# Modulation of two token streams with the weights as TensorE's stationary operand, the gate's third computed later

## What is computed

```python
silu_c, silu_cc = jax.nn.silu(c), jax.nn.silu(c_ctx)          # two vectors of 1024
for l in range(DEPTH):                                        # DEPTH = 2
    mod_x = silu_c  @ w_ada[l] + b_ada[l]                     # w_ada[l]: 1024 x 3072
    mod_c = silu_cc @ w_ada[l] + b_ada[l]
    shift, scale, gate = jnp.split(mod, 3, axis=-1)           # for x and for the context
    h = rmsnorm(x, g_pre) * (1.0 + scale) + shift             # before the input projection
    y = merge(branches(h)) @ w_out                            # attention, conv, retention, Fourier
    x = x + gate * rmsnorm(y, g_post)                         # at the end of the layer
```

## Time and profile before

| | us |
|---|---|
| median of three runs | 2798.82 |
| lowest and highest run | 2790.05, 2798.84 |
| the profiled execution | 2791.78 |
| its span (first to last instruction) | 2790.0 |
| busy PE, loads of stationary operands (PEld) | 2569.3 (92%), 2123.9 (76%) |
| busy DVE, ACT, POOL | 1123.0, 1083.0, 1292.2 |
| mean granted TensorE clock | 0.974 |

### The profile page before, as it was taken

How to read it: one execution, slowest core, us unless ns; L and a number is a source line. 1 busy time by engine, 2 the same in 40 slices (tenths; PEclk the granted TensorE clock), 3 DMA queues, 4 the chain that set the end, 5 groups by cost and what they waited for, 6 DMA issues and landing times.

```text
span 2790.0 us, 39335 instructions
## 1 busy us (share of the span) xinstructions
PE 2569.3 (92%) x13000; PEld 2123.9 (76%) x13000; DVE 1123.0 (40%) x1675; ACT 1083.0 (39%) x2170; POOL 1292.2 (46%) x1012
## 2 busy tenths in 40 slices
PE   7888969988999899999999869888999899999998
PEld 2777957777888778888887358777888678888886
DVE  2453446386244233333331356474244323333322
ACT  2644553375212443333332333574212433343332
POOL 1667952365222355555554132464222455556553
PEclk9999989999999999999999979999998999999999
DMA  5346642100121143344336431000210233344333
GB/s 230 100 119 187 189 162 61 31 1 13 45 64 29 56 122 109 111 132 146 109 110 236 160 99 48 19 1 25 63 39 25 83 114 112 109 132 146 110 109 121
DMA packets 387918, 270.48 MB, mean 97 GB/s; under 512 B 15452, under 2 KB 360668, under 8 KB 385252
## 3 DMA queue, kind: packets, MB, share of 16 engines
q1 hardware_dynamic: 373792, 231.26, 27.5%
q10 hardware_dynamic: 14024, 37.88, 3.8%
HBM read 259.63 MB, written 9.45 MB: 96 GB/s over the span
## 4 chain that ended last, share of the span: by engine, by line
PE 58%; issue 19%; POOL 14%; DVE 5%; ACT 3%; POOLq 1%; DMA 0%; DVEq 0%; ACTq 0%; SPq 0%
PE ps L596 56%; POOL w_lo L509 14%; DVE a_probT_lo L1346 2%; PE ps L742 1%; ACT a_probT_hi L1130 1%; DVE a_out_sum L1346 1%; DVE norm_tmp L1423 1%; DVE hT_lo L1346 1%; DMA w_ada<-in_w_ada 0%; DVE r_prev L1616 0%; PE ps L694 0%; POOLq L508 0%; ACT square_junk L973 0%; PE ps L632 0%; ACT a_prob L1119 0%
## 5 line engine op out<-in xcount | busy, mean ns | idle before, releaser
L509 POOL TENSOR_TENSOR w_lo<-w_raw,w_hi 128x512 fp32r<-128x512 f32 x786 | 1055.3, 1350 | 1115.1 <-ACT w_hi L973 1104.8
L596 PE MATMUL ps<-hT_hi,w_hi 128*128 128x512 f32 (+1 forms) x2528 | 943.7, 373 | 50.6 <-POOL w_lo L509 27.0
L596 PE MATMUL ps<-hT_hi,w_lo 128*128 128x512 f32 (+1 forms) x2528 | 932.4, 369 | 0.0
L596 PE MATMUL ps<-hT_lo,w_hi 128*128 128x512 f32 (+1 forms) x2528 | 932.3, 369 | 0.0
L973 ACT ACTIVATE w_hi<-w_raw 128x512 fp32r<-128x512 f32 x786 | 492.0, 630 | 1063.5 <-PE ps L596 883.3
L596 PEld LDWEIGHTS ps<-hT_hi,w_hi 128*128 128x128 f32 x2528 | 481.1, 190 | 141.7 <-POOL w_lo L509 22.9
L596 PEld LDWEIGHTS ps<-hT_hi,w_lo 128*128 128x128 f32 x2528 | 481.6, 190 | 78.7
L596 PEld LDWEIGHTS ps<-hT_lo,w_hi 128*128 128x128 f32 x2528 | 482.0, 191 | 76.5
L1346 DVE TENSOR_TENSOR merge_tmp<-merge_tmp,ps 128x512 f32<-128x512 f32 (+1 forms) x160 | 101.4, 634 | 683.3 <-PE ps L596 601.1
L547 POOL TENSOR_TENSOR a_prob<-a_prob,softmax_stats 128x640 f32<-128x640 f32 (+2 forms) x144 | 163.7, 1137 | 142.5 <-DVE softmax_stats L1532 141.9
L1346 DVE TENSOR_TENSOR merge_tmp<-merge_tmp 128x512 f32<-128x512 f32 (+1 forms) x120 | 182.2, 1518 | 4.1
(11 more groups left out here) (195 smaller groups left out, 2783.3 us busy)
## 6 DMA issues: line engine op xcount, KB each, us to landing
w_raw<-in_w_in SPq DMA_DIRECT2D x512, 256.0 KB, 2.9
w_raw<-in_w_o_rest SPq DMA_DIRECT2D x120, 256.0 KB, 2.7
w_ada<-in_w_ada SPq DMA_DIRECT2D x16, 1536.0 KB, 9.3
w_raw<-in_w_out SPq DMA_DIRECT2D x80, 256.0 KB, 2.9
w_raw<-in_w_o_attn SPq DMA_DIRECT2D x40, 256.0 KB, 2.7
w_raw<-in_dft_x SPq DMA_DIRECT2D x32, 256.0 KB, 2.7
gate_row<-gate_rows ACTq DMA_DIRECT2D x5, 512.0 KB, 3.7
x_tile_first<-in_x ACTq DMA_DIRECT2D x4, 512.0 KB, 6.4
```

Of the source, the lines that this page charges most:

```text
L509: eng.tensor_tensor(w_lo[:, r, :], raw[:, r, :], w_hi[:, r, :].bitcast(F32), ALU.subtract).then_inc(sem["w_split"], tally.up("w_split"))
L596: return eng.matmul(dst, lhsT, rhs, start=start, stop=stop)
```

## The change

w_ada becomes the stationary operand and the two silu columns the moving one. PE does the shift and the scale first: 16 blocks of 128 output columns times 8 row blocks, 128 matmuls of two moving columns each. The row blocks are summed in PSUM in pairs, each pair in a bank of its own (4 to 7), and DVE adds the four banks (`mod_sumT`). The results lie as columns at once, so the 16 transposes, `mod_rows` and the wait for them are gone. The bias and norm_post come as columns as well.

SP requests 128x2048 (1 MB) for each row block, in layer 1 all eight during the multiplication by w_out. The gate's third comes as eight loads of 0.5 MB (`ada_gate`) into the part of `hT` that the context doesn't use; the first four wait until three pairs of PE's modulation are done, the last four until all are. PE's part for the gate (`gate_columns`, 64 matmuls) stands behind the first two tiles of the context's projection, `gate_turn` four tiles later. DVE's `gate_made` and ACT's `gate_save` follow. PE's modulation of layer 1 now waits for the first half of w_out's results alone (banks 4 to 7), and the tokens are requested ahead of the small loads.

```diff
-ADA_AHEAD = 5
+ADA_AT = (2, 4, 6, 8, 10, 12, 14, 15)
...
             def ada(layer, k):
                 if k > 1:
-                    eng.wait_ge(ada_in[k - 2], 16 * (layer + 1))
-                eng.dma_start(w_ada[:, k, :], a["w_ada"][layer][k * P:(k + 1) * P, :]).then_inc(ada_in[k], 16)
+                    eng.wait_ge(ada_in[k - 2], 32 * layer + 16)
+                eng.dma_start(w_ada[:, k, :], a["w_ada"][layer][k * P:(k + 1) * P, 0:2 * D]).then_inc(ada_in[k], 16)
+
+            def ada_gate(layer, k):
+                eng.wait_ge(sem["mod_used"], KT // 2 * layer + KT // 4 + k // 4 + 1)
+                if k > 1:
+                    eng.wait_ge(ada_in[k - 2], 32 * layer + 32)
+                eng.dma_start(w_gate[:, :, k, 512:1024], a["w_ada"][layer][k * P:(k + 1) * P, 2 * D:3 * D]
+                              .rearrange("p (h n) -> p h n", h=2)).then_inc(ada_in[k], 16)
...
                 else:
-                    eng.wait_ge(sem["y_out"], tally.now("y_out"))
+                    eng.wait_ge(sem["y_out"], tally.now("y_out", -4))
+                for part in range(KT // 2):
+                    for k in range(2):
+                        eng.wait_ge(ada_in[2 * part + k], 32 * l + 16)
+                    for c in range(2 * KT):
+                        for k in range(2 * part, 2 * part + 2):
+                            last = mm(ps[:, 4 + part, 2 * c:2 * c + 2], w_ada[:, k, c * P:(c + 1) * P], sT[:, :, k],
+                                      k % 2 == 0, k % 2 == 1)
+                    last.then_inc(sem["mod_used"], tally.up("mod_used"))
+
+            def gate_columns(l):
                 for k in range(KT):
-                    eng.wait_ge(ada_in[k], 16 * (l + 1))
-                    for n in range(6):
-                        ins = mm(ps[0:2, n, :], sT[:, :, k], w_ada[:, k, n * 512:(n + 1) * 512], k == 0, k == KT - 1)
...
-                eng.wait_ge(sem["mod_saved"], tally.take("mod_saved", 6))
-                for c in range(2 * KT):
-                    last = eng.transpose(ps[:, 6, 2 * c:2 * c + 2], m_rows[0:2, c * P:(c + 1) * P], ident[0:2, 0:2])
-                last.then_inc(sem["mod_cols"], tally.up("mod_cols"))
+                    eng.wait_ge(ada_in[k], 32 * l + 32)
+                for c in range(KT):
+                    for k in range(KT):
+                        last = mm(ps[:, 7, 2 * c:2 * c + 2], w_gate[:, c // 4, k, 512 + c % 4 * P:512 + (c % 4 + 1) * P],
+                                  sT[:, :, k], k == 0, k == KT - 1)
+                last.then_inc(sem["gate_cols"], tally.up("gate_cols"))
...
                 if not p.full:
                     project(p, 2, True)
+                    gate_columns(p.layer)
                     turn_values(p, A_V, None)
                     project(p, 4)
+                    gate_turn()
...
-                project(p, 6, True)
+                if p.ctx:
+                    project(p, 2, True)
+                    gate_columns(p.layer)
+                    project(p, 4)
+                    gate_turn()
...
-                for n in range(6):
-                    eng.wait_ge(sem["mod_rows"], tally.take("mod_rows"))
-                    c = slice(n * 512, (n + 1) * 512)
-                    tt(m_rows[0:2, c], ps[0:2, n, :], m_bias[0:2, c], ALU.add).then_inc(sem["mod_saved"], tally.up("mod_saved"))
...
+                eng.wait_ge(sem["mod_used"], tally.take("mod_used", KT // 2))
+                eng.tensor_reduce(m_sum[:, :], ps[:, 4:8, 0:4 * KT].rearrange("p a n -> p n a"), AX.X, ALU.add).then_inc(
+                    sem["dve_own"], tally.up("dve_own"))
```

More of the change, by code:

```diff
@@ L207, in trunk @@
         turned = at("rope_turned", [P, SEQ], W + 12288)
[L209 to L213, removed]
+        w_ada = at("w_ada", [P, KT, 2 * D], 0)
+        m_sum = at("mod_sumT", [P, 4 * KT], W)
+        w_gate = at("w_ada_gate", [P, 2, KT, SEQ], 0)
         x_first = at("x_tile_first", [P, 4, D], Z + 4096)
@@ L440, in ada @@
                 if k > 1:
-                    eng.wait_ge(ada_in[k - 2], 16 * (layer + 1))
-                eng.dma_start(w_ada[:, k, :], a["w_ada"][layer][k * P:(k + 1) * P, :]).then_inc(ada_in[k], 16)
-            def modulation(p):
[L445 to L449, removed]
+                    eng.wait_ge(ada_in[k - 2], 32 * layer + 16)
[6 more added lines that the diff above has]
+                              .rearrange("p (h n) -> p h n", h=2)).then_inc(ada_in[k], 16)
+            def modulation(p):
+                if p.layer == 0:
+                    for k in range(KT):
+                        ada(0, k)
+                for k in range(KT):
+                    ada_gate(p.layer, k)
             def fourier(p):
@@ L1294, in _ @@
                     root(after, 0)
+                    gate_save(p.layer)
                     stage_end(eng, tally, "act")
@@ L1301, in _ @@
                 tile_range(p, A_Q, A_Z)
-                if not p.ctx:
+                if p.ctx:
+                    gate_save(p.layer)
+                else:
                     values_high(p)
@@ L1395, in modulation, with gate_made @@
+                for s in range(2):
+                    eng.scalar_tensor_tensor(mod[:, s, 0, :], mod[:, s, 0, :], 1.0, gpre[:, :],
                                                   ALU.add, ALU.mult).then_inc(sem["dve_own"], tally.up("dve_own"))
                 eng.wait_ge(sem["dve_own"], tally.now("dve_own"))
+            def gate_made():
+                eng.wait_ge(sem["gate_cols"], tally.take("gate_cols"))
+                cols = ps[:, 7, 0:2 * KT].rearrange("p (k s) -> p k s", s=2)
+                for s in range(2):
+                    tt(g_cols[:, s * KT:(s + 1) * KT], cols[:, :, s], b_cols[:, 2 * KT:3 * KT], ALU.add).then_inc(sem["dve_own"], tally.up("dve_own"))
+                eng.wait_ge(sem["dve_own"], tally.now("dve_own"))
+                for s in range(2):
+                    ins = tt(g_cols[:, s * KT:(s + 1) * KT], g_cols[:, s * KT:(s + 1) * KT], gpost[:, :])
+                    ins.then_inc(sem["gate_made"], tally.up("gate_made")) if s else ins.then_inc(sem["dve_own"], tally.up("dve_own"))
@@ L1781, in _ @@
                     a_keys(p)
+                    gate_made()
                     r_keys(p)
@@ L1792, in _ @@
                 for t in range(4):
+                    if p.ctx and t == 2:
+                        gate_made()
                     split_queries(p, t)
@@ L1818, in _ @@
                 stage_end(eng, tally, "dve")
-INPUTS = ("x", "ctx", "w_ada", "b_ada", "norm_post", "w_in", "attn_sink", "ret_decay", "w_o_attn", "w_out")
+INPUTS = ("x", "ctx", "w_ada", "w_in", "attn_sink", "ret_decay", "w_o_attn", "w_out")
 TABLES = ("rope", "dft_x", "dft_c", "dft_head", "mask", "ident", "ret", "small")
```

50 lines of the change are left out of this document (32 added, 18 removed).

## The result

The changed kernel takes 2862.38 us (median of five runs, 2850.12 to 2865.81), the kernel before 2798.69 in the same job (2788.60 to 2798.84): a ratio of 1.0228, 95% interval 1.0209 to 1.0248. The profiled execution of the changed kernel is its fastest, 2850.12 us, with a span of 2848.3 and a mean granted clock of 0.960 (0.974 before). Against the profiled execution before that is +58.3 us.

What follows compares the result with a forecast made beforehand. PE was taken to bound the kernel (busy 92%), so added PE work costs its full length. 10.9 + 2.0 + 47.8 - 1 + 0.3 = +60 on 2791.8, plus 3 for run spread: 2855 us; own range 2836 to 2878, given 2812 to 2880.

Steps and rivals of the forecast that it cites:

- The price of a record: New w_ada streams on PE: each record bound by its load, 0.101 us at full clock, 0.214 at the lower.
- The lower bound of 0.067: Cheapest possible record in the w_ada streams, 0.067 us, read from small transposes of 128 columns.
- The clock: New two-column streams run at 0.50 where they start cold and fall to 0.50 where they start warm.
- Rival 1: In all new streams back-to-back records keep the clock up; 2787 to 2791 us, no change; chance 0.08.
- Layer 0, shift and scale: Head of layer 0: 256 records at 0.214 us, `norm_tmp` at 68.0 instead of 57.1, +10.9 us.
- DVE's tail: Layer 0, from PE's end of shift and scale to `norm_tmp`: 1.6 us, where it was 2.4 before.
- Layer 1: Shift and scale there: PE starts at 1540.3 instead of 1544.2, `norm_tmp` at 1591.7 instead of 1589.7, +2.0 us.
- The gate: Behind two projection tiles in each layer: 22.4 us of stream plus 1.5 of cold restart, +23.9 a layer, +47.8.
- the 1 us that I had given back there: Layer 1's tiles: some of PE's 1.1 us idle time filled because the four-unit ring is full, -1 us.
- The 44: Streams starting warm: 44 records at the full clock, 4.4 us, before the clock falls to 0.50.
- The restart: Tiles behind the gate's stream start cold: 16 records 0.094 us dearer each, 1.5 us a layer.
- SP's queue and the fifth unit: Layer 0: w_in's fifth unit requested near 72 behind the gate's loads, hidden by 30 us, otherwise some 3 us.

Runs made afterwards that it cites:

- e_gate_eighth: Changed kernel with the gate's stream cut to one row block of eight, 16 records instead of 128; 2813.33 us, ratio 1.0055 to the kernel before.
- e_cols128: Changed kernel with the two silu columns repeated to 128 moving columns in all w_ada streams, same loads; 2788.59 us, ratio 0.9964 to the kernel before.
- e_cols64: Changed kernel with the two silu columns repeated to 64 moving columns in all w_ada streams, same loads; 2807.34 us (one run).
- e_mod128: Changed kernel with 128 moving columns in shift and scale only, two left in the gate; 2822.15 us (one run).
- e_raise64: Changed kernel with 128 moving columns in the first quarter of shift and scale, 64 in the rest and the gate; 2788.21 us, ratio 0.9983 to before.
- e_rows: Changed kernel with only the operand swap undone, w_ada moving in rows of 512 again; 2793.12 us, ratio 0.9991 to the kernel before.

## Why the prediction was right

Forecast 2855, measured 2862.38, inside the range and inside the forecast's own; the direction and the mechanism held: long streams of loads with two columns run at 0.50 and cost their full length on PE. That the sum lies within 2 us of the profiled execution (2851.8 against 2850.12) is luck in part, as the last point shows. By its steps:

- **The price of a record.** 0.214 us at the low clock was measured to the digit (54.74 us for 256). At the full clock the 16 records with two columns are 0.106 us apart (e_gate_eighth) and those with 128 columns 0.111 (e_cols128), where I took 0.101 from eight retention records. With the last one's tail it is 14.40 us for 128, 0.1125 (64 columns, e_cols64). The Trainium skill (TensorE: Matmul & The Clock Gate, LDWEIGHTS) makes an estimate of 107 ns; the full-clock rows lie within 5% of it, and the slow rows at twice that, which a price by columns alone doesn't say. The lower bound of 0.067, from transposes with two rows, never applied.
- **The clock.** Right for two columns, and it decides everything: e_cols128 and e_mod128 show it by the width alone. That loads were busy 3.49 of 3.70 us didn't show that they set the pace, since PE was busy 3.68 of them too; e_cols64 shows it. My argument for it was looser than its result, since the 64-column row spoke only for a stream that starts cold (e_cols64, e_raise64). Had the kernel streamed 64 columns, the same argument would have priced three of four streams wrongly.
- **Rival 1**, that a busy PE keeps its clock. The rows refute it: 100% busy and 0.50. The Trainium skill's rule (the same page, Why this matters for your kernels), read literally, would have kept these streams at 1.00; here a busy share of PE did not tell whether the clock holds.
- **Layer 0, shift and scale: +10.9 forecast, +11.4 measured.** PE started 1.07 us later, because two row blocks must have landed; I had costed that at nothing. With the same loads e_rows, which needs one block, starts at 10.51. DVE's tail was 1.1 us and not 1.6.
- **Layer 1: +2.0 forecast.** From the end of w_out to `norm_tmp` the difference grows from 35.9 to 38.6, +2.7. PE started right behind w_out as said, and DVE's chain was ready 18.6 us early. The 1.3 us that PE's wait within w_out got shorter are no term of my sum.
- **The gate: +23.9 a layer forecast.** The stream itself took 23.8 us (22.4 forecast). From `norm_tmp` to the stage behind it the difference grows by 26.0 in layer 0 (37.4 less 11.4) and by 25.1 in layer 1 (63.8 less 38.6, after the 1 us that I had given back there). Some 35 records ran at the full clock instead of 44: 23.8 = 35 x 0.1125 + 93 x 0.214. The 44 came from a stretch behind w_out in which PE had almost nothing to do, not from a stream of loads. The restart, with what else the tiles lose or win, is what is left, 2.2 and 1.3 us for 1.5 forecast. This is the mis-sized term, some 2 us each.
- **SP's queue and the fifth unit.** Hidden as said: the unit was requested at 73.4 and PE did not wait for it behind the gate.
- **Not foreseen:** the 6.4 us won back in retention. Up to there the difference had grown to 65.4, against my 60; the profiled execution ended at +58.3, so the nearness of that number is in part luck. The median lies 12.3 us above the profiled execution, where I had added 3.

## What to carry to other kernels

Before making weights stationary for a very narrow moving operand, count the loads and price them at the lower clock: most of the 384 records in a layer took 0.21 us each for two useful columns, although PE looked 100% busy. If the loads must stay, repeating the columns costs little (0.106 us a record with two columns and 0.111 with 128 at the full clock, from start to start) and can keep the clock. Work moved into PE's idle time is free only if nothing on another engine starts from what stands behind it.

## What the hardware showed that I had not expected

- The clock's course depended on its own state: with 64 columns the last 192 records ran at the pace of 0.50 in one kernel's head (e_cols64) and at that of 1.00 in another's (e_raise64), where 64 records with 128 columns preceded them.
- Two columns lost the full clock in each of the six long streams that began with it, after some 27 to 44 records (from the lengths, at 0.1125 and 0.214 us), with PE and its loads 100% busy. The two short ones of 16 records kept it (e_gate_eighth).
- Retention's stretch, with matmuls of 64, 128 and 512 columns, ran mostly at half the clock in both profiles of the kernel before, at 2122 to 2146. The same work behind the same wait of 2.0 us lost only one stretch of 0.79 in the changed kernel. This is a swing of some 6 us in a stage that the change doesn't touch, and every version that was compared with before has it.
